# A two-phase MLP with block products: another assignment of tiles, input sums, squares and weight sums to engines

## The chip, the cores and the metric

The kernel runs on one core of a Trainium2 chip. The metric is the device time of one execution in microseconds (us), the median of several runs. PE (TensorE) multiplies, DVE (VectorE), ACT (ScalarE) and POOL (GpSimd) work element by element, SP (SyncE) issues transfers. PE writes into eight PSUM banks; POOL cannot read them.

## What is computed

A trunk of two layers on an input of 1024 rows by 1024 columns. Each layer has a mixer (attention of one kind or another), a norm, and an MLP. The change lies in the MLP and in the norm ahead of it:

```python
def rms_norm(x, g):
    y = xf * lax.rsqrt(jnp.mean(xf * xf, axis=-1, keepdims=True) + EPS)
    return (y * g).astype(x.dtype)

def sqrelu_mlp(xn, w1, w2):
    return jnp.square(jax.nn.relu(xn @ w1)) @ w2

for i in range(DEPTH):                       # 2 layers
    ...
    h = h + rms_norm(mix, g[1])
    f = sqrelu_mlp(rms_norm(h, g[2]), ffn_w1[i], ffn_w2[i])   # 1024 -> 4096 -> 1024
    h = h + rms_norm(f, g[3])
```

## The kernel before

**Precision.** Every fp32 operand of a product is split into a high part (rounded, by ACT) and a low part (the difference, by DVE or POOL), and each product is three matmuls: high x high, high x low, low x high. A low half can only be written after its high half.

**Two phases.** The hidden layer has 32 tiles of 128 columns. Phase one makes them (x @ w1, relu, square), phase two multiplies them by w2. Four tiles are made as plain products in `project_first` (two halves of 512 rows each, `th` 0 and 1); the other 28 come in 14 pairs. A pair is made as a 2x2 block product with seven products in place of eight (Strassen's scheme in Winograd's form): its operands are blocks of x and w1 and sums of blocks. `LOOPS = 6` turns of a loop make two pairs each (p = 0 into h_even, p = 1 into h_odd), and a peeled last turn makes the last two.

**Input sums.** x_sums holds four blocks: first four raw blocks of the transposed, normed input (high plus low: three made by POOL in `raw`, the fourth by DVE), then sums of them by DVE in place, then ACT's high and DVE's low halves of the four sums.

**Weights of phase one.** For each product k of a pair ACT writes the high half of its w1 operand (`up_high`) and POOL the low half (`up_low`); POOL also makes four sums of w1 blocks per pair. The halves go into a ring of eight slots; `w1_slot_free` says which product must be done before a slot is rewritten.

**Evacuation.** PE's products go round four banks. In `pair` DVE adds the seven products up into the four hidden blocks of the pair, frees the banks (`a_free`), squares each block by a fused op (max with 0, times itself), then makes three sums of squared blocks plus one in place: these are the seven block operands that phase two wants of a pair. SP stores all seven to h_operand_scratch. The squares and sums of a pair stand ahead of the next pair's evacuation in DVE's queue.

**Which tiles go where.** The four plain tiles and the first twelve pairs enter phase two as block operands: the plain tiles are put together into two pairs, with eight sums by DVE (`first_sum` into h_last_rows and h_more) before the loop. The last two pairs get no sums; their four tiles come last in phase two, as plain products (`down_last`).

**Phase two.** Products z = 0 to 27 in four groups g of seven (r = 0 to 6), four pairs deep in the first three groups and two in the last. For each z ACT copies the high half of the h operand and of the w2 operand, DVE the low half of h (`h_low`), POOL the low half of w2 (`down_low`); POOL also makes four sums of w2 blocks per group (`down_sum`). DVE takes PE's results into acc (`take`). The w2 operand buffers are three, so a half for z is written when product z-3 is done.

**The norm ahead** (`last_chunk_and_norm` on DVE, `norm` on ACT): DVE finishes the mixer's output (adds), scales it (y), adds the residual (h) and scales it for the MLP (xn); ACT makes the sums of squares and the roots. PE transposes the first 512 rows, runs the four tiles on them, transposes the last 512 and runs the four tiles again; ACT copies the high half of each transposed tile and DVE the low half.

Everything is ordered by semaphores; each engine runs its own queue in order. The order of operations is written out by hand.

## Time and profile before

| | |
|---|---|
| time, median of 3 runs | 2703.27 us (2702.24 to 2703.44) |
| the profiled execution | 2701.42 us, its span 2699.6 us |
| PE busy | 2454.9 us, 91% |
| DVE, POOL, ACT busy | 72%, 58%, 39% |
| mean granted clock of PE | 0.962 of full |

The profile comes from one execution. Its span starts at its first instruction; times below count from there. "Idle before" an instruction is the time in which its engine did nothing, and behind the arrow stands what ended it. The MLP of layer 0 lies at about 955 to 1635 us, that of layer 1 at 2009 to 2700 us.

### The profile page before, as it was taken

How to read it: one execution, taken by the hardware profiler on the slowest of the kernel's cores; microseconds unless marked ns; L12 is line 12 of the kernel's file. 1: busy time of each engine (PE TensorE's matmuls, PEld its weight loads, DVE VectorE, ACT ScalarE, POOL GpSimd, SP SyncE). 2: the span in 40 equal slices, each digit the busy share in tenths (PEclk: the TensorE clock that was granted, in tenths of full speed). 3: DMA queues.
4: the chain of work that ended last, by engine and by line, in shares of the span. 5: the costliest groups of instructions: out<-in, count | busy, mean ns of one | idle time of the engine just before them, and what ended most of it. 6: DMA issues, size and time to landing. Idle time of an engine off the chain costs nothing. (4 is left out here: it accounts for less than half of the span.)

```text
span 2699.6 us, 34715 instructions
## 1 busy us (share of the span) xinstructions
PE 2454.9 (91%) x11680; PEld 2017.9 (75%) x11680; DVE 1938.1 (72%) x3041; ACT 1046.8 (39%) x1785; POOL 1569.2 (58%) x833
## 2 busy tenths in 40 slices
PE   7899998898898987999999999977897999999998
PEld 6689877676776875888777887866775788878786
DVE  5599999766665588888755576165569788777666
ACT  5443533556554352122333235165544121233231
POOL 2112777545444156898877632366627698777951
PEclk9899989899999998999999999989998999999999
DMA  4471734543444623545644344654451554654343
GB/s 145 67 112 30 165 95 143 161 110 83 144 122 153 226 63 113 157 143 160 221 155 157 131 132 136 151 144 120 125 172 47 169 159 142 226 192 141 103 139 125
DMA packets 324033, 369.62 MB, mean 137 GB/s; under 512 B 14434, under 2 KB 222338, under 8 KB 321588
## 3 DMA queue, kind: packets, MB, share of 16 engines
q1 hardware_dynamic: 314404, 350.38, 44.3%
q10 hardware_dynamic: 9216, 16.78, 2.1%
q8 instruction: 83, 1.36, 0.2%
q0 software_dynamic: 272, 0.62, 0.1%
q14 instruction: 58, 0.48, 0.1%
HBM read 237.18 MB, written 130.55 MB: 136 GB/s over the span
## 5 line engine op out<-in xcount | busy, mean ns | idle before, releaser
L443 PE MATMUL ps<-xn_T,w_split 128*128 128x512 f32 (+1 forms) x2928 | 684.8, 393 | 32.4 <-DVE h_even L2264 30.8
L443 PEld LDWEIGHTS ps<-xn_T,w_split 128*128 128x128 f32 (+1 forms) x2928 | 551.7, 189 | 152.6 <-DVE h_even L2264 31.6
L443 PE MATMUL ps<-w_operand,h_operand 128*128 128x512 f32 x2016 | 468.1, 394 | 26.6 <-issue 17.0
L399 POOL TENSOR_TENSOR w_split<-w_raw,w_split 128x1024 fp32r<-128x1024 f32 x80 | 197.2, 2476 | 484.7 <-ACT w_split L392 484.4
L443 PEld LDWEIGHTS ps<-w_operand,h_operand 128*128 128x128 f32 x2016 | 383.6, 191 | 110.8 <-issue 29.0
L1193 POOL TENSOR_TENSOR w_split<-w_raw,w_split 128x512 fp32r<-128x512 f32 x168 | 271.9, 1643 | 74.5 <-ACT w_split L1670 74.5
L2315 DVE TENSOR_TENSOR acc<-acc,ps 128x512 f32<-128x512 f32 x288 | 186.1, 681 | 153.2 <-PE ps L443 152.7
L443 PE MATMUL ps<-x_sums_high,w_split 128*128 128x512 f32 x896 | 287.4, 392 | 4.3 <-POOL w_split L1193 4.3
L1225 POOL TENSOR_TENSOR w_operand<-w_block,w_operand 128x2048 fp32r<-128x2048 f32 x42 | 222.8, 5309 | 99.5 <-ACT w_operand L1690 99.5
L443 PE MATMUL ps<-w_split,hidden 128*128 128x512 f32 x960 | 224.7, 395 | 9.0 <-POOL w_split L399 6.3
L1677 ACT ACTIVATE h_operand<-h_operand_raw 128x2048 fp32r<-128x2048 f32 (+1 forms) x56 | 95.4, 1704 | 332.8 <-DMA h_operand_raw<-h_operand_scratch 332.8
L443 PEld LDWEIGHTS ps<-w_split,hidden 128*128 128x128 f32 x960 | 182.3, 191 | 48.7 <-issue 6.7
L443 PEld LDWEIGHTS ps<-x_sums_high,w_split 128*128 128x128 f32 x896 | 169.9, 190 | 40.7 <-ACT h_last_rows L1653 5.1
L2236 DVE TENSOR_TENSOR h_operand<-h_operand_raw,h_operand 128x2048 fp32r<-128x2048 f32 (+1 forms) x56 | 173.0, 3089 | 35.9 <-ACT h_operand L1677 35.6
L1670 ACT ACTIVATE w_split<-w_raw 128x512 fp32r<-128x512 f32 x168 | 99.4, 624 | 216.4 <-PE ps L443 201.6
L443 PE MATMUL ps<-w_split,unit_tile 128*128 128x512 f32 x576 | 158.9, 408 | 18.8 <-issue 7.4
L443 PE MATMUL ps<-x_sums_low,w_split 128*128 128x512 f32 x448 | 175.6, 392 | 0.0
L1959 DVE MATCH_REPLACE8 masks<-max,masks 128x1024 f32<-128x1024 f32 (+2 forms) x192 | 167.1, 880 | 0.1
L1955 DVE MAX8 max<-masks 128x8 f32<-128x1024 f32 (+2 forms) x192 | 161.4, 884 | 0.5 <-DVEq L1965 0.5
L443 PE MATMUL ps<-k_split,q_tile 128*128 128x192 f32 (+4 forms) x640 | 136.6, 340 | 23.1 <-DMA q_tile<-q_scratch 15.6
L2069 DVE TENSOR_TENSOR probs_T<-ps,probs_T 128x512 fp32r<-128x512 f32 x144 | 98.9, 688 | 75.5 <-ACT probs_T L1578 74.5
L1578 ACT ACTIVATE probs_T<-ps 128x512 fp32r<-128x512 f32 x144 | 83.9, 594 | 149.6 <-PE ps L2528 148.7
(249 smaller groups left out, 4333.4 us busy)
## 6 DMA issues: line engine op xcount, KB each, us to landing
h_operand_raw<-h_operand_scratch SPq DMA_DIRECT2D x42, 1024.0 KB, 5.2
w_raw<-in_w SPq DMA_DIRECT2D x72, 512.0 KB, 8.0
w_block<-in_w SPq DMA_DIRECT2D x48, 512.0 KB, 6.3
q_scratch<-q_split SPq DMA_DIRECT2D x128, 128.0 KB, 2.5
q_tile<-q_scratch ACTq DMA_DIRECT2D x64, 256.0 KB, 2.7
cat_scratch<-attn_out_split SPq DMA_DIRECT2D x128, 128.0 KB, 2.7
w_raw<-in_w_in SPq DMA_DIRECT2D x30, 512.0 KB, 5.0
h_operand_scratch<-h_even SPq DMA_DIRECT2D x14, 1024.0 KB, 4.5
```

Source lines behind the costliest of these rows:

```text
L399: nc.gpsimd.tensor_tensor(whl[:, n0 % 4, 1, :], wraw[:, n0 % 4, :], whl[:, n0 % 4, 0, :].bitcast(F32), ALU.subtract).then_inc(w_lo, 1)
L443: return nc.tensor.matmul(out_ap, stat, mov, start=start, stop=stop)
L1193: nc.gpsimd.tensor_tensor(w1_split(L, k, 1), w1_operand(L, k), w1_split(L, k, 0).bitcast(F32), ALU.subtract).then_inc(w1_lo, 1)
L1225: nc.gpsimd.tensor_tensor(w_split2(z, 1), w_operand2(z), w_split2(z, 0).bitcast(F32), ALU.subtract).then_inc(w2_lo, 1)
L1578: nc.scalar.activation(pT[:, x % 4, 0, :], ps[:, 4 + y % 2, :], ACT.Copy).then_inc(c_hi, 1)
L1670: nc.scalar.activation(w1_split(L, k, 0), w1_operand(L, k), ACT.Copy).then_inc(w1_hi, 1)
L1677: nc.scalar.activation(h_split(z, 0), h_split(z, 1, raw=True), ACT.Copy).then_inc(h2_hi, 1)
L1955: nc.vector.max(m8[:, e], rows[e]).then_inc(tk, 1)
L1959: nc.vector.match_replace(rows[e], m8[:, e], rows[e], NEG_SEL).then_inc(tk, 1)
L2069: nc.vector.tensor_tensor(pT[:, x % 4, 1, :], ps[:, 4 + y % 2, :], pT[:, x % 4, 0, :].bitcast(F32), ALU.subtract).then_inc(c_free, 1)
L2236: nc.vector.tensor_tensor(h_split(z, 1), h_split(z, 1, raw=True), h_split(z, 0).bitcast(F32), ALU.subtract).then_inc(h2_lo, 1)
L2315: last = nc.vector.tensor_tensor(e, e, o, ALU.add)
```

## The change

1. The four plain tiles come last in phase two, as plain products; all 14 pairs of phase one enter it as block operands. `first_sum` goes, SP moves the plain tiles with two stores in place of fourteen, the last two pairs get their squares and sums like the others, and the last one is put into h_end, a buffer of its own over the input sums. The rows of w2 are indexed accordingly.
2. POOL makes no input sum. DVE makes the raw block of the upper-left tiles inside the norm (`first_raw`) and the one of the lower-left after the transposes; ACT writes the other two straight from PSUM (`xn_raw`), reading the transposed tiles a second time, and PE waits for that before it overwrites their banks.
3. The squares of the pairs are ACT's: a relu and a square per block in place of DVE's fused op. DVE waits for them (h_sq), after the evacuation of the pair's last product.
4. w1's ring of halves has seven slots, and each is free when the product seven before is done.
5. In phase two POOL makes the sums of w2 in another order among themselves and against the low halves; SP loads w2's fourth block of group 0 after the second h operand.

```diff
-UP_RING = [-3, -3, -2, -2, -1, 0, 0, 0]
+UP_RING = [-3, -3, -2, -2, -1, -1, 0]
...
-        return w2[lay, (24 + j) * P:(25 + j) * P, :]
+        return w2[lay, (j - 4) * P:(j - 3) * P, :]
...
                 pe.wait_ge(a_free, f - 3)
+                if s % 2:
+                    pe.wait_ge(x_hi, 24 * (s // 2) + (9 if th else 1) + j)
                 project_half(FIRST[s] + j, f, th,
...
-        c = (k + 2 * L["tf"]) % 8
+        c = (k % 7 + 2 * L["tf"]) % 8
...
-        return up_group(L, k - 7 if k >= 8 else UP_RING[k])
+        return up_group(L, UP_RING[k] if first and k < 7 else k - 6)
...
-        raw(0, 0, 0)
-        raw(1, 0, 4)
-        pool.wait_ge(a_free, trans_pos(sn, 1, KT - 1) + 1)
-        raw(3, 1, 4)
-        head(0)
+        head(0, True)
...
+        def xn_raw(s, th, j):
+            for kt in range(4, KT):
+                f = trans_pos(s, th, kt)
+                act.wait_ge(a_free, f + 1)
+                nc.scalar.activation(xsum[:, j, kt - 4, :], ps[:, f % 4, :], ACT.Identity,
+                                     scale=gcol[:, s, kt:kt + 1]).then_inc(x_hi, 1)
...
             split_hi(act, FIRST[s] + 1)
+            if s % 2:
+                act.wait_ge(u_done, 3 * (s - 1) + 2)
+                xn_raw(s, 0, 1)
...
                 adds(7)
+                if s % 2:
+                    first_raw(s, 0)
                 stage_a(3)
+                if s % 2:
+                    first_raw(s, 1)
                 stage_b(2)
...
+        def squares_of(p, o, blocks, i, last=False):
+            act.wait_ge(a_free, up_group(L, 7 * p + o) + 1 + 14 * i)
+            n = 112 * lay + 8 * p + {1: 0, 5: 2, 6: 6}[o]
+            for j in blocks:
+                nc.scalar.activation(h_block(p, j, last), h_block(p, j, last), ACT.Relu).then_inc(h_sq, 1)
+            for m, j in enumerate(blocks):
+                act.wait_ge(h_sq, n + m + 1 + 16 * i)
+                nc.scalar.activation(h_block(p, j, last), h_block(p, j, last), ACT.Square).then_inc(h_sq, 1)
+
+        def round_(i, last=False):
+            for o in range(14):
+                if o < 7:
+                    up_high(7 + o, i)
+                elif not last:
+                    up_high(o - 7, i + 1)
+                if o % 7 == 1:
+                    squares_of(o // 7, 1, (1,), i, last)
+                if last and o == 12:
+                    down_high(0)
+                if o % 7 == 5:
+                    squares_of(o // 7, 5, (3, 0), i, last)
+                if o % 7 == 6:
+                    squares_of(o // 7, 6, (2,), i, last)
...
             nc.vector.tensor_tensor(b[1], b[0], o1, ALU.add).then_inc(a_free, 1)
-            done_to(1)
-            square(p, 1, i)
...
-            square(p, 3, i)
-            square(p, 0, i)
-            if not last:
-                ok_to(3)
-                nc.vector.tensor_tensor(b[0], b[1], b[0], ALU.subtract).then_inc(h_ok, 1)
...
+            nc.vector.tensor_tensor(b[2], b[2], m6, ALU.subtract).then_inc(a_free, 1)
+            squared(6)
+            nc.vector.tensor_tensor(b[0], b[1], b[0], ALU.subtract).then_inc(h_ok, 1)
+            sum_to(1)
+            nc.vector.tensor_tensor(b[4], b[3], b[0], ALU.subtract).then_inc(h_ok, 1)
+            sum_to(2)
+            nc.vector.tensor_tensor(b[5], b[4], b[1], ALU.add).then_inc(h_ok, 1)
+            squared(8)
+            nc.vector.tensor_tensor(b[6], b[4], b[2], ALU.subtract).then_inc(h_ok, 1)
...
-        sp.wait_ge(h0_ok, 18 * lay + 18)
+        sp.wait_ge(x_hi, 24 * lay + 24)
+        for th in range(2):
+            sp.dma_start(hopd[lay, 14 + th, 0:4].rearrange("k r t -> r k t"), (first_rows, last_rows)[th][:]).then_inc(h0_mv, 16)
...
             down_low(z)
+            if g == 0:
+                down_low(z + 1)
             pool.wait_ge(w2_ld[1], w_loads(lay, g))
             pool.wait_ge(w2_ld[3], w_loads(lay, g))
             down_sum(g, 0, b12, b22, b12, ALU.subtract)
-            if g == 0:
-                down_low(z + 1)
-            down_sum(g, 1, b11, b12, b11, ALU.add)
             if g:
                 down_low(z + 1)
             down_low(z + 2)
-            down_sum(g, 2, b21, b11, b21, ALU.subtract)
+            down_sum(g, 1, b11, b12, b11, ALU.add)
             down_low(z + 3)
-            down_sum(g, 3, b22, b22, b11, ALU.subtract)
-            for r in range(4, 7):
-                down_low(z + r)
+            down_sum(g, 2, b22, b22, b11, ALU.subtract)
+            down_low(z + 4)
+            down_sum(g, 3, b21, b11, b21, ALU.subtract)
+            down_low(z + 5)
+            down_low(z + 6)
```

**How the instructions move.** DVE, layer 0, from its input sums to the end of what stands ahead of the loop of pairs. Before:

```order
L2219 TENSOR_TENSOR x_sums<-x_sums 128x1024 x4
L2210 TENSOR_TENSOR h_last_rows<-h_first_rows,h_last_rows 128x512
L2219 TENSOR_TENSOR x_sums<-x_sums 128x1024 x4
L2210 TENSOR_TENSOR h_last_rows<-h_first_rows,h_last_rows 128x512
L2227 TENSOR_TENSOR x_sums_low<-x_sums,x_sums_high_89 128x1024 x2
L2227 TENSOR_TENSOR x_sums_low<-x_sums,x_sums_high_91 128x1024 x2
L2210 TENSOR_TENSOR h_last_rows<-h_last_rows 128x512
L2210 TENSOR_TENSOR h_last_rows<-h_last_rows,h_first_rows 128x512 x2
L2227 TENSOR_TENSOR x_sums_low<-x_sums,x_sums_high_92 128x1024 x2
L2227 TENSOR_TENSOR x_sums_low<-x_sums,x_sums_high_90 128x1024 x2
L2210 TENSOR_TENSOR h_last_rows<-h_last_rows 128x512
L2210 TENSOR_TENSOR h_more<-h_last_rows,h_first_rows 128x512 x2
```

and after the change, from the low halves of the second transposes on:

```order
L1786 TENSOR_SCALAR xn<-acc,rstd_b 128x8x128 x2
L1906 SCALAR_TENSOR_TENSOR xn_T<-ps,gain_cols,xn_T 128x512 x8
L2334 TENSOR_TENSOR x_sums<-xn_T 128x1024 x2
L2244 TENSOR_TENSOR x_sums<-x_sums 128x1024 x8
L2252 TENSOR_TENSOR x_sums_low<-x_sums,x_sums_high_89 128x1024 x2
L2252 TENSOR_TENSOR x_sums_low<-x_sums,x_sums_high_91 128x1024 x2
L2252 TENSOR_TENSOR x_sums_low<-x_sums,x_sums_high_92 128x1024 x2
L2252 TENSOR_TENSOR x_sums_low<-x_sums,x_sums_high_90 128x1024 x2
```

The eight operations on h_last_rows and h_more are gone from between the sums and the low halves, and the low halves follow the sums directly.

ACT, layer 0, end of phase one and start of phase two (w_operand and h_operand are phase two's operands; the number tells the buffer). Before:

```order
L1670 ACTIVATE w_split<-w_split_raw 128x512
L1670 ACTIVATE w_split<-w_raw 128x512 x4
L1690 ACTIVATE w_operand_107<-w_block_113 128x2048
L1677 ACTIVATE h_operand_101<-h_operand_raw_104 128x2048
L1690 ACTIVATE w_operand_108<-w_block_115 128x2048
L1677 ACTIVATE h_operand_102<-h_operand_raw_105 128x2048
L1677 ACTIVATE h_operand_103<-h_operand_raw_106 128x2048
```

and after the change:

```order
L1721 ACTIVATE h_even<-h_even 128x512
L1724 ACTIVATE h_even<-h_even 128x512
L1721 ACTIVATE h_end<-h_end 128x512
L1724 ACTIVATE h_end<-h_end 128x512
L1689 ACTIVATE w_operand_108<-w_block_114 128x2048
L1676 ACTIVATE h_operand_102<-h_operand_raw_105 128x2048
L1721 ACTIVATE h_end<-h_end 128x512 x2
L1724 ACTIVATE h_end<-h_end 128x512 x2
L1721 ACTIVATE h_end<-h_end 128x512
L1724 ACTIVATE h_end<-h_end 128x512
L1689 ACTIVATE w_operand_109<-w_block_116 128x2048
L1676 ACTIVATE h_operand_103<-h_operand_raw_106 128x2048
```

The high half of the second w2 operand (w_operand_108 before, w_operand_109 now) stands behind the relus and squares of the last pair.

POOL, layer 0, the first group of phase two and the start of the second. L1225 (L1218 now) writes a low half, L1231 (L1224 now) a sum of w2 blocks; blocks 113 to 116 are 114 to 117 in the changed kernel. Before:

```order
L1225 TENSOR_TENSOR w_operand_107<-w_block_113,w_operand_107 128x2048
L1231 TENSOR_TENSOR w_block_114<-w_block_116,w_block_114 128x2048
L1225 TENSOR_TENSOR w_operand_108<-w_block_115,w_operand_108 128x2048
L1231 TENSOR_TENSOR w_block_113<-w_block_114,w_block_113 128x2048
L1225 TENSOR_TENSOR w_operand_109<-w_block_114,w_operand_109 128x2048
L1231 TENSOR_TENSOR w_block_115<-w_block_113,w_block_115 128x2048
L1225 TENSOR_TENSOR w_operand_107<-w_block_116,w_operand_107 128x2048
L1231 TENSOR_TENSOR w_block_116<-w_block_116,w_block_113 128x2048
L1225 TENSOR_TENSOR w_operand_108<-w_block_116,w_operand_108 128x2048
L1225 TENSOR_TENSOR w_operand_109<-w_block_115,w_operand_109 128x2048
L1225 TENSOR_TENSOR w_operand_107<-w_block_113,w_operand_107 128x2048
L1225 TENSOR_TENSOR w_operand_108<-w_block_113,w_operand_108 128x2048
```

and after the change:

```order
L1218 TENSOR_TENSOR w_operand_108<-w_block_114,w_operand_108 128x2048
L1218 TENSOR_TENSOR w_operand_109<-w_block_116,w_operand_109 128x2048
L1224 TENSOR_TENSOR w_block_115<-w_block_117,w_block_115 128x2048
L1218 TENSOR_TENSOR w_operand_110<-w_block_115,w_operand_110 128x2048
L1224 TENSOR_TENSOR w_block_114<-w_block_115,w_block_114 128x2048
L1218 TENSOR_TENSOR w_operand_108<-w_block_117,w_operand_108 128x2048
L1224 TENSOR_TENSOR w_block_117<-w_block_117,w_block_114 128x2048
L1218 TENSOR_TENSOR w_operand_109<-w_block_117,w_operand_109 128x2048
L1224 TENSOR_TENSOR w_block_116<-w_block_114,w_block_116 128x2048
L1218 TENSOR_TENSOR w_operand_110<-w_block_116,w_operand_110 128x2048
L1218 TENSOR_TENSOR w_operand_108<-w_block_114,w_operand_108 128x2048
L1218 TENSOR_TENSOR w_operand_109<-w_block_114,w_operand_109 128x2048
```

In group 0 every sum now stands one low half later than before, and in the second group the second low half stands ahead of the second sum. The sums of blocks 115 and 116 have changed places: the sixth low half reads the sum that is now made last.

## Rows read from the trace of the kernel before

**Rows 1.** the page's part 1: busy us (share of the span) xinstructions
```profile
PE 2454.9 (91%) x11680; PEld 2017.9 (75%) x11680; DVE 1938.1 (72%) x3041; ACT 1046.8 (39%) x1785; POOL 1569.2 (58%) x833
```

**Rows 2.** PE's waits, whole span: engine, what waits, releaser: us in total, times, longest
```profile
PE ps L558 <- DVE xn L1763: 34.1, 3, 15.9
PE ps L443 <- DVE h_even L2264: 30.8, 2, 15.4
```

**Rows 3.** PE's timeline, start of layer 0's MLP: start, us, instruction xcount [idle before]
```profile
954.91 22.04 PE L443 MATMUL ps<-xn_T,w_split 128*128 128x512 f32 x96 [0.49 <-DVE xn_T L1871]
986.07 6.28 PE L558 MATMUL ps<-ident,xn 128*128 128x128 f32 x32 [9.12 <-DVE xn L1763]
992.17 27.48 PE L443 MATMUL ps<-xn_T,w_split 128*128 128x512 f32 x120
1021.84 0.59 PE L443 MATMUL ps<-x_sums_high,w_split 128*128 128x512 f32 x1 [2.19 <-POOL w_split L1193]
...
1044.55 5.25 PE L443 MATMUL ps<-xn_T,w_split 128*128 128x512 f32 x12 [15.38 <-DVE h_even L2264]
```

**Rows 4.** DVE's timeline, the norm in front of that MLP
```profile
967.10 4.62 DVE L1783 SCALAR_TENSOR_TENSOR acc<-acc,rstd_a,gain_rows 128x1024 f32<-128x1024 f32 x2
971.64 6.76 DVE L1794 TENSOR_TENSOR acc<-acc,h_in 128x1024 f32<-128x1024 f32 x2
978.32 5.58 DVE L1763 TENSOR_SCALAR xn<-acc,rstd_b 128x1024 f32<-128x1024 f32 x2
...
984.60 1.42 DVE L1763 TENSOR_SCALAR xn<-acc,rstd_b 128x1024 f32<-128x1024 f32 x2
```

**Rows 5.** POOL's timeline, the same stretch
```profile
970.60 12.76 POOL L1184 TENSOR_TENSOR x_sums<-xn_T 128x1024 f32<-128x1024 f32 x4
```

**Rows 6.** DVE's timeline, where the input sums begin and where phase one's first evacuation stands
```profile
1001.16 6.99 DVE L2219 TENSOR_TENSOR x_sums<-x_sums 128x1024 f32<-128x1024 f32 x4 [2.28 <-POOL x_sums L1184]
...
1043.82 0.68 DVE L2264 COPY h_even<-ps 128x512 f32<-128x512 f32 x1
```

**Rows 7.** DVE's groups, 994 to 1044.5 us: xcount | busy, mean ns | idle
```profile
L2227 DVE TENSOR_TENSOR x_sums_low<-x_sums,x_sums_high 128x1024 fp32r<-128x1024 f32 x8 | 15.7, 2014 | 0.0
...
L2210 DVE TENSOR_TENSOR h_last_rows<-h_last_rows 128x512 f32<-128x512 f32 x2 | 3.5, 1756 | 0.0
L2210 DVE TENSOR_TENSOR h_last_rows<-h_last_rows,h_first_rows 128x512 f32<-128x512 f32 x2 | 3.4, 1716 | 0.0
L2210 DVE TENSOR_TENSOR h_more<-h_last_rows,h_first_rows 128x512 f32<-128x512 f32 x2 | 3.3, 1690 | 0.0
L2210 DVE TENSOR_TENSOR h_last_rows<-h_first_rows,h_last_rows 128x512 f32<-128x512 f32 x2 | 2.5, 1232 | 0.0
```

**Rows 8.** tile x_sums: duration ns min/median/max, first and last start
```profile
L2219 DVE TENSOR_TENSOR x_sums<-x_sums x16: 1210/2303/2318, 1001.2 to 2070.9; 128x1024 f32<-128x1024 f32 x16
```

**Rows 9.** tile h_first_rows: ScalarE's square, ns min/median/max
```profile
L1655 ACT ACTIVATE h_first_rows<-h_first_rows x8: 629/630/630, 980.5 to 2038.3; 128x512 f32<-128x512 f32 x8
```

**Rows 10.** all engines, phase one at speed: us, busy (xcount) by engine, PEclk, DMA
```profile
1064.00:1292.00 228.00, 228.00 (x1008) 188.79 (x1006) 186.90 (x189) 51.20 (x85) 198.05 (x132) 1.00 0.52 154
```

**Rows 11.** ACT's groups in the same stretch
```profile
L1670 ACT ACTIVATE w_split<-w_split_raw 128x512 fp32r<-128x512 f32 x12 | 7.6, 633 | 84.1 <-POOL w_split_raw L1189 84.1
```

**Rows 12.** PE's timeline, hand-over from phase one to two, layer 0
```profile
1316.03 5.71 PE L443 MATMUL ps<-w_operand,h_operand 128*128 128x512 f32 x24 [2.33 <-DVE acc L2313]
```

**Rows 13.** PE's timeline, the same hand-over in layer 1
```profile
2374.70 79.19 PE L443 MATMUL ps<-w_operand,h_operand 128*128 128x512 f32 x336 [6.48 <-DVE acc L2313]
```

**Rows 14.** POOL's groups, 1302 to 1360 us, first products of phase two
```profile
L1225 POOL TENSOR_TENSOR w_operand<-w_block,w_operand 128x2048 fp32r<-128x2048 f32 x5 | 27.6, 5524 | 2.0 <-ACT w_operand L1690 2.0
L1231 POOL TENSOR_TENSOR w_block<-w_block,w_block 128x2048 f32<-128x2048 f32 x4 | 24.9, 6233 | 6.3 <-DMA w_block<-in_w 6.3
```

**Rows 15.** PE's timeline, the three holes between groups of phase two
```profile
1399.70 20.58 PE L443 MATMUL ps<-w_operand,h_operand 128*128 128x512 f32 x80 [5.50 <-issue]
...
1482.56 17.76 PE L443 MATMUL ps<-w_operand,h_operand 128*128 128x512 f32 x70 [4.26 <-issue]
...
2537.56 32.74 PE L443 MATMUL ps<-w_operand,h_operand 128*128 128x512 f32 x136 [6.70 <-issue]
```

**Rows 16.** POOL's timeline in front of the first of them
```profile
1381.69 11.39 POOL L1231 TENSOR_TENSOR w_block<-w_block,w_block 128x2048 f32<-128x2048 f32 x2
1393.04 11.10 POOL L1225 TENSOR_TENSOR w_operand<-w_block,w_operand 128x2048 fp32r<-128x2048 f32 x2
```

235 lines of the change are left out of this document (96 added, 139 removed).

## The prediction

> **What bounds the kernel now.** I read the page's busy shares first, then PE's waits, then the timelines of PE, DVE and POOL around each wait. PE is busy 91% of the span [rows 1], and the change neither adds nor removes a matmul, so it can only give or take PE's holes. The 128x512 matmuls run back to back wherever nothing holds them: in the steady part of phase one PE is busy 228.00 of 228.00 us with 1008 of them, 0.226 us each, at a granted clock of 1.00, the 2.4 GHz level [rows 10]. So a product of 12 is 2.71 us, a first-tile half of 24 is 5.43, and a product of phase two (48) is 10.86. The holes that touch the change stand in four places, the first three once per layer:
> (a) Before the second transposes PE waits 9.1 us for DVE's scaled rows (two of the three waits in 34.1 us) [rows 2, 3].
> (b) Four products into phase one, PE waits 2.2 us for POOL's low half and then 15.4 us for DVE, which comes to its first evacuation only at 1043.82 [rows 2, 3, 6].
> (c) At the hand-over to phase two PE waits for DVE 2.3 us in layer 0 and 6.5 in layer 1 [rows 12, 13].
> (d) Inside phase two there are three holes of 5.50, 4.26 and 6.70 us [rows 15] that the profile calls issue. The first ends where the first of POOL's two low halves must end: POOL writes two weight sums (11.39 us) and only then the low half that the second product of the group needs [rows 16].
>
> **The change part by part, (a).** Today POOL adds four raw input sums from 970.60 to 983.36 [rows 5]. While it does, DVE's y, h and xn take 2.31, 3.38 and 2.79 us each; xn takes 0.71 once POOL is quiet [rows 4]. A sum of the same width takes 1.21 alone and 2.30 beside POOL [rows 8]. Now DVE and ScalarE alone make these sums. I price y and h at 1.21 and xn at 0.71 with POOL quiet, one y still at 2.3 because POOL's last weight split stays: 2.3+1.2+2.4+1.4 = 7.3 us for two y, two h and two xn that took 16.96. The remaining ScalarE root and two xn add about 3 us. All rows are then ready some 9 to 10 us earlier, at 977 instead of 986.0, which is when PE's first half ends (954.91+22.04). The two raw sums that DVE takes over (2 x 1.21) fall into its two waits for ScalarE's roots, ahead of 967.10. So hole (a) goes to about 0. What is late next is ScalarE.
> The Trainium skill, page "SBUF — State Buffer", section "Who interferes with whom", says why: an instruction of VectorE with two SBUF inputs, or in a 2-port mode, and one of GpSimd exclude each other for a whole instruction. The drop of xn from 2.79 to 0.71 us agrees. If the slow times were instead DVE's own, hole (a) would stay; that is rival C.
>
> **(a), what is added on PE's path.** ScalarE reads the upper four transposed tiles once more (4 ops per half), and PE's first product in that bank waits for it. An op of this width takes 0.63 us there [rows 9]. First half: +0.7 us. Second half: the reads stand behind all eight high copies, so PE starts about 8.0 us after its first transpose instead of 6.1 (992.17-986.07) [rows 3]: +1.9.
>
> **(b).** Between its last transposed tile and its first evacuation DVE now runs 26 ops, among them eight sums of first tiles, 12.7 us in all [rows 7]. These go, since the first four tiles are no longer part of the block sums. The wait for POOL's raw sums (2.28 us) [rows 6] goes too. What remains on DVE is 2 raw sums, 8 sums, 8 lows: 10 x 1.21 with POOL quiet, then 8 x 2.0 beside POOL's low halves [rows 7] = 28.1 us. PE meanwhile has 4 half tiles and 4 products, 21.7+10.9 = 32.6 us. DVE has about 8 us of transposed tiles in front of it, just as PE has, so it arrives 4 us before PE needs the fifth bank: the 15.4 goes, at least to 0 to 2. As for the 2.2 us for POOL: from the second half tile on, two ScalarE ops and two copies (2.5 us) and six POOL ops of at most 2 us stand in front of the low half of the third product, 14.5 us, and PE reaches that product 16.3 us behind the tile (2 x 5.43 + 2 x 2.71). So it goes as well.
> Sum of (a) and (b), from the end of the first half (976.95) to the start of the fifth product: now 1044.55-976.95 = 67.6 us; then 0.7+8.0+21.7+10.9 = 41.3. That saves 26.3. Behind the hole the first 12 matmuls take 5.25 us in place of 2.71 [rows 3], another 2.5. **28.8 us a layer, 57.6 for both.** Bounds: 20 (half of the DVE lows late) to 31.
>
> **Steady phase one.** Per pair of products four fused squares leave DVE and eight ops of 0.63 us come to ScalarE, 5.0 us in a pair of 19.0; ScalarE is busy 51 of 228 us now, DVE 187 [rows 10]. DVE's block sums now wait for ScalarE's squares, and the next pair's evacuation stands behind those sums in DVE's queue. Worked out from the sixth product's end: DVE 1.4, ScalarE 2.6, then the seventh product, four sums: DVE is free 4.3 us after the pair's last product, or 7 if POOL doubles the sums. PE needs the first bank of the next pair 10.2 us after it. So it costs nothing while 3 to 6 us of slack stand. In the first pair ScalarE is held by POOL's weight sum, which is behind there: **0 to 2 us, I take 1 a layer, 2 for both.** The ring of weight halves is 7 deep in place of 8, or 4 to 6 at the loop's turn, and POOL has 30 of 228 us to spare: nothing.
> The Trainium skill, "ScalarE: Activation LUTs", section "Rules for kernel authors", says that relu belongs on VectorE. Here it would be right for the op by itself: relu and square are 1.26 us on ScalarE against one fused op. If it held for the path too, rival D is what it would do here, with its own price; by the slack above it shows only in the last pair of a layer.
>
> **(c) The hand-over** gets worse. Today POOL makes the first weight sum while phase one ends. Now its second low half comes first, and that waits for a ScalarE copy which stands behind the last squares: about 5 us (bounds 3 to 8) after phase two starts. From there to the low half of the sixth product are nine POOL ops and three hand-overs through ScalarE. Nine ops took 52.5 us, 5.83 each, and a hand-over 2.0 [rows 14]. So 5+52.5+6 = 63.5 us, and PE wants it after 5 x 10.86 = 54.3: 9 us of holes in place of 2.3 and 6.5. At 5.0 us an op and an early start it is 2, at 8 us start 12. DVE has sums in the last pair too, but POOL is idle just then. **Cost 9.4 us for both; bounds -5 to +15.**
>
> **(d)** In later groups the second low half moves ahead of the second sum, one POOL op, about 5.7 us (11.39/2) [rows 16]. 5.50+4.26+6.70 = 16.5 of holes become 0 to 1 each: **gain 15.4**, bounds 11 to 16.5. The sixth product's low half gets one hand-over (2.0) more but has 3 us to spare.
>
> Moves that cost nothing: 14 small stores of first tiles become 2, and both pairs of the end store seven blocks, 0.75 MB more each while PE multiplies; the fourth w2 block is loaded behind the second h operand on SP's queue, which only follows the order of use. The eight small loads of the last tiles become two and go one product later, with eight products still before ScalarE copies them.
> Sum: 57.6 - 2 - 9.4 + 15.4 = 61.6 us. From the profiled execution's 2701.42 (span 2699.6) that is 2639.8; the median is 1.85 higher, 2703.27, so **2641.6 us**.
>
> **Rivals.**
> A, POOL's chain is the new bound: hand-overs cost 12 us each layer (15 worse than now, not 9.4), the holes of (d) keep 2 us each, and the first pairs 2. 57.6-4-15+10 = 48.6: 2655. For it: POOL's 5.83 mean [rows 14]; against: DVE has fewer two-input ops there.
> B, everything fits: hand-over no worse than today, 57.6-0-0+16 = 73.6: 2630. For it: POOL is idle when the last squares run, and DVE's sums then cost 0.7 us each.
> C, hole (a) stays, because y, h and xn are slow by themselves: 6.4 us less per layer (9.1 less the part that ScalarE's four first-tile squares now take anyway), 2654.
> D, slower than before: the handshake of DVE and ScalarE. In the steady part ScalarE waits 7.0 us per pair for POOL's weight sum (84.1 us in 12) [rows 11]. Should that wait fall in front of the third and first squares, DVE is free at 11 to 13 us instead of 4.3 to 7 and PE, which decides at 10.2, stops in every one of 28 pairs: at 2.5 us a pair 70 us, 2712. Against: the sum in question is made two to four products earlier, since POOL starts it when product 2 ends.
> E, the order is as written but DVE's first lows are slowed to 2.3 and start late, so that the 15.4 shrinks only to 6: 2653.
>
> **How the numbers follow.** Forecast 60%, 2630 to 2652 by its bounds; A 13%; B 8%; C 7%; E 6%; D 3%; the rest 3% lies beyond, on the good side. Range **2624 to 2663**. This kernel's measurement can tell 0.2%, 5.4 us, from no change. Faster 0.96, same 0.01, slower 0.03.
>
> **What would show it.** Right: no PE wait for xn over 2 us before the second transposes; PE starts the second half about 8 us behind its first transpose; no wait for h_even at the fifth product; xn, y and h at 0.7 and 1.2 us; 228-like full busy PE in phase one; holes of 2 to 12 us, ended by POOL's w_operand, within the first six products of phase two; none over 1 us at the second product of a later group. Wrong: a wait of PE for an h block in every pair (D), or xn still at 2.8 us with POOL quiet (C).

## The result and the profile after

The changed kernel takes **2620.52 us** (median of 4 runs, 2619.45 to 2623.67) against 2702.76 for the kernel before beside it (2698.99 to 2703.44): ratio 0.970, 95% interval 0.9684 to 0.9717. The forecast was 2641.6 in a range of 2624 to 2663: the sign was right, the gain of 82 us was 20 more than the 61.6 forecast, and the time lies 3.5 us below the range. A second measurement (e11 below) gave 2624.14 (2621.12 to 2627.58), ratio 0.9715 (0.9699 to 0.9731), so the low end of the range is where the kernel stands; the centre was 17 to 21 us off.

I cut the span at four points of PE's timeline: A is from the first matmul of an MLP's input projection to the first of phase two, B from there to the next norm's first projection (in layer 1 to the end), M lies between the two MLPs. The first five columns are differences of such row starts, in us; the last two are the profiled execution's span and the median of all executions.

| kernel | A, layer 0 | B, layer 0 | M | A, layer 1 | B, layer 1 | span | median |
|---|---|---|---|---|---|---|---|
| before | 347.7 | 332.7 | 373.9 | 347.9 | 342.4 | 2699.6 | 2702.8 |
| changed | 318.2 | 321.1 | 370.7 | 318.3 | 332.9 | 2617.6 | 2620.5 |
| changed, again (e11) | 318.2 | 322.1 | 372.3 | 318.3 | 333.0 | 2622.4 | 2624.1 |
| e1 raw sums on GpSimd | 333.4 | 320.8 | 372.3 | 333.9 | 330.2 | 2647.8 | 2648.4 |
| e4 eight first sums added | 331.2 | 323.7 | 372.2 | 329.0 | 332.8 | 2644.2 | 2646.5 |
| e8 four first sums added | 323.5 | 323.7 | 371.5 | 323.9 | 331.3 | 2630.0 | 2630.5 |
| e2 squares on VectorE | 320.0 | 323.4 | 372.2 | 321.1 | 333.0 | 2626.0 | 2628.1 |
| e3 old weight order | 318.2 | 340.4 | 371.6 | 320.0 | 348.7 | 2655.1 | 2656.2 |
| e7 first group's old start | 318.2 | 324.4 | 372.3 | 318.2 | 333.1 | 2620.7 | 2623.4 |
| e5 before, new order alone | 347.9 | 321.5 | 371.8 | 347.8 | 327.5 | 2673.5 | 2675.1 |

Of the 82.0 us between the two spans 59.1 are in the two A, 21.3 in the two B (20.1 by the second measurement), and 1.6 in M and what lies ahead of the first MLP together. M is anything from 370.7 to 374.1 in the experiments, and e5, which changes nothing there, has 371.8 where the kernel before has 373.9, so its 3.2 are no effect of the change. PE's timeline of the changed kernel at the start of layer 0's MLP, to be laid beside [rows 3]:

```profile
956.48 22.05 PE L442 MATMUL ps<-xn_T,w_split 128*128 128x512 f32 x96 [1.30 <-ACT x_sums L1309]
...
981.24 2.63 PE L559 MATMUL ps<-ident,xn 128*128 128x128 f32 x16 [0.97 <-DVE xn_T L1906]
985.32 27.49 PE L442 MATMUL ps<-xn_T,w_split 128*128 128x512 f32 x120 [1.45 <-ACT x_sums L1309]
```

The hole of 9.12 us ahead of the second transposes is gone, ScalarE's second reading of the transposed tiles adds the waits of 1.30 and 1.45, and behind them the next row with an idle time of any size is the first of phase two (0.78); 2.19 and 15.38 are gone too. VectorE's timeline in the norm, beside [rows 4], and where phase one's first evacuation stands, beside [rows 6, 7]:

```profile
968.74 2.48 DVE L1806 SCALAR_TENSOR_TENSOR acc<-acc,rstd_a,gain_rows 128x1024 f32<-128x1024 f32 x2
971.14 2.35 DVE L1825 TENSOR_TENSOR acc<-acc,h_in 128x1024 f32<-128x1024 f32 x2
973.41 1.41 DVE L1786 TENSOR_SCALAR xn<-acc,rstd_b 128x1024 f32<-128x1024 f32 x2
```

```profile
997.51 16.89 DVE L2252 TENSOR_TENSOR x_sums_low<-x_sums,x_sums_high 128x1024 fp32r<-128x1024 f32 x8
1014.32 0.68 DVE L2286 COPY h_even<-ps 128x512 f32<-128x512 f32 x1
```

y, h and xn take 1.24, 1.18 and 0.71 us each (2.31, 3.38, 2.79 before), and the evacuation starts at 1014.32 instead of 1043.82. PE's waits over the whole span (total, times, longest), beside [rows 2], and its timeline at the two hand-overs, beside [rows 12, 13]; there is no hole between the groups of phase two where [rows 15] had three:

```profile
PE ps L442 <- issue: 14.9, 3, 7.6
...
PE ps L442 <- DVE acc L2325: 6.8, 2, 3.4
...
PE ps L442 <- ACT x_sums L1309: 5.5, 4, 1.4
```

```profile
1274.70 11.18 PE L442 MATMUL ps<-w_operand,h_operand 128*128 128x512 f32 x48 [0.78 <-DVE h_operand L2257]
1289.27 90.92 PE L442 MATMUL ps<-w_operand,h_operand 128*128 128x512 f32 x387 [3.39 <-DVE acc L2325]
```

```profile
2299.32 45.44 PE L442 MATMUL ps<-w_operand,h_operand 128*128 128x512 f32 x192 [3.40 <-DVE acc L2325]
2346.82 63.46 PE L442 MATMUL ps<-w_operand,h_operand 128*128 128x512 f32 x272 [2.06 <-issue]
```

### The profile page after: what moved, and what is told of

Read it like the earlier page. It is cut to its first block, busy times and chain, and to the rows that moved or that the text cites. A ratio compares the mean times of both kernels' runs of the same rounds, so it can differ in the third digit from the quotient of the medians.

```text
span 2617.6 us, 34947 instructions
## 1 busy us (share of the span) xinstructions
PE 2432.2 (93%) x11680; PEld 1999.3 (76%) x11680; DVE 1761.4 (67%) x2933; ACT 1189.7 (45%) x2025; POOL 1471.8 (56%) x821
## 4 chain that ended last, share of the span: by engine, by line
PE 66%; issue 14%; DVE 9%; POOL 5%; ACT 4%; DMA 2%; DVEq 1%; SPq 0%; POOLq 0%; ACTq 0%
PE ps L442 63%; POOL attn_out_split L1164 2%; POOL attn_out L1162 2%; PE ps L2528 1%; DVE masks L1994 1%; DVE max L1990 1%; DVE probs_T L2104 1%; DVE logits L2069 1%; DVE masks L1973 1%; POOL attn_out_split L1160 1%; DMA h_operand_raw<-h_operand_scratch 1%; ACT relu_scores L1426 1%; ACT probs_T L1577 1%; POOL attn_out_low L1157 1%; DVE acc L1806 1%
## 5 line engine op out<-in xcount | busy, mean ns | idle before, releaser
L1186 POOL TENSOR_TENSOR w_split<-w_raw,w_split 128x512 fp32r<-128x512 f32 x168 | 241.8, 1450 | 104.9 <-ACT w_split L1669 103.4
L1218 POOL TENSOR_TENSOR w_operand<-w_block,w_operand 128x2048 fp32r<-128x2048 f32 x42 | 207.8, 4947 | 111.4 <-ACT w_operand L1689 111.4
L2257 DVE TENSOR_TENSOR h_operand<-h_operand_raw,h_operand 128x2048 fp32r<-128x2048 f32 (+1 forms) x56 | 167.5, 2991 | 52.8 <-ACT h_operand L1676 52.5
L1669 ACT ACTIVATE w_split<-w_raw 128x512 fp32r<-128x512 f32 x168 | 104.9, 629 | 167.4 <-PE ps L442 163.8
```

Of the source, the lines that this page charges most:

```text
L1186: nc.gpsimd.tensor_tensor(w1_split(L, k, 1), w1_operand(L, k), w1_split(L, k, 0).bitcast(F32), ALU.subtract).then_inc(w1_lo, 1)
L1218: nc.gpsimd.tensor_tensor(w_split2(z, 1), w_operand2(z), w_split2(z, 0).bitcast(F32), ALU.subtract).then_inc(w2_lo, 1)
L1669: nc.scalar.activation(w1_split(L, k, 0), w1_operand(L, k), ACT.Copy).then_inc(w1_hi, 1)
L2257: nc.vector.tensor_tensor(h_split(z, 1), h_split(z, 1, raw=True), h_split(z, 0).bitcast(F32), ALU.subtract).then_inc(h2_lo, 1)
```

## The experiments

Each run is compared with runs of the kernel before on the same chip (medians 2699.2 to 2703.0). "Over the changed kernel" counts from its first measurement, 2620.5; from the second, 2624.1, each such number is 3.6 us less.

**Part (a), who makes the raw input sums.** e1 gives the six raw sums of a layer back to GpSimd:

```diff
+        raw(0, 0, 0)
+        raw(1, 0, 4)
...
+        raw(3, 1, 4)
...
-                xn_raw(s, 0, 1)
...
-        xn_raw(sn, 1, 3)
...
-                    first_raw(s, 0)
...
-                    first_raw(s, 1)
```

> The changed kernel, but the six raw input sums of a layer are on GpSimd again, where the kernel before had them; everything else stays. Theory S (GpSimd's sums held up VectorE's norm work): the y, h and xn rows of VectorE that took 2.48, 2.35 and 1.41 for two go back to about twice to three times that, PE's gap ahead of the second half's transposes grows from 6.8 to 14 to 15 us in each layer, and the time is 2620.5 + 2 x 7.9 = 2636 us (2633 to 2640). Rival C (those rows were slow for another reason, or the second half was late for another reason): gap stays near 7, time 2619 to 2622.

Measured: 2648.41, ratio 0.980 (0.978 to 0.982), 28 us over the changed kernel. VectorE's norm rows and PE's timeline of e1:

```profile
969.37 4.62 DVE L1813 SCALAR_TENSOR_TENSOR acc<-acc,rstd_a,gain_rows 128x1024 f32<-128x1024 f32 x2
973.92 6.74 DVE L1832 TENSOR_TENSOR acc<-acc,h_in 128x1024 f32<-128x1024 f32 x2
980.58 5.59 DVE L1793 TENSOR_SCALAR xn<-acc,rstd_b 128x1024 f32<-128x1024 f32 x2
```

```profile
988.35 6.18 PE L557 MATMUL ps<-ident,xn 128*128 128x128 f32 x32 [9.11 <-DVE xn L1793]
...
1026.12 0.79 PE L442 MATMUL ps<-x_sums_high,w_split 128*128 128x512 f32 x1 [4.15 <-POOL w_split L1184]
```

The rows are those of [rows 4] again, 4.62, 6.74 and 5.59, with nothing changed in these steps themselves: GpSimd's sums made them slow, and rival C is out. The hole is back (9.11), and a second one that I had not counted, 4.15 for GpSimd's low half, since its first weight sums now stand behind the raw ones. Per layer: holes of 9.1 and 4.15, less the 0.97 and 1.45 that go with ScalarE's reads, are 10.8 us; A grew by 15.2 and 15.7. The other 4.4 and 4.9 us are matmuls that take longer behind a hole: the granted clock is 0.50 from 988 to 992 us and again from 1026 to 1030. The time lies 8 us over the 2640 at which my range ended, since I had counted neither the second hole nor this.

**Part (b), the sums of the first tiles.** e4 puts eight unused VectorE sums where the kernel before had those of the first tiles, e8 four:

```diff
+        extra(0)
         x_sum_op(3, 3, 0, ALU.subtract, s0)
...
+        extra(2, 3, 4)
         x_sum_low(19, 3)
         x_sum_low(21, 1)
+        extra(5, 6, 7)
```

> The changed kernel with work added: eight VectorE sums of 128x512 in each layer at the places where the kernel before had the sums of the first four tiles (one and one among the x sums, three and three among the low parts). Their results are not used. Theory B1 (these sums, in VectorE's order ahead of the first product's copy, made the first pair wait): the copy that starts at 1014.3 comes 5.6 us (8 x 0.7) to 12.7 us (the four rows of before) later; PE has 3 us to spare there, so it waits 3 to 10 us ahead of the fifth product in each layer: 2626 to 2640 us, most likely 2634. Rival B2 (the slow low parts under GpSimd were all of it): 2620 to 2622.

> As e4_first_sums_added, with four extra VectorE sums of 128x512 in place of eight (one ahead of each of the four places). Each of the four left out took 1.74 us there, 7 us in all, of a hole of 8.88 us, so 1.9 us of hole is left in each layer. In e4 the stage grew by 12.9 us for that hole, so 4.0 us were slower matmuls. Theory L (the loss at a lower granted clock comes only behind long holes): 2620.5 + 2 x 1.9 = 2624 us (2622 to 2627). Theory A (any hole at that place costs the same 4 us behind it): 2632 us (2630 to 2635).

Measured: e4 2646.51, ratio 0.9808 (0.9785 to 0.9832), 26 us over the changed kernel; e8 2630.51, ratio 0.9743 (0.9728 to 0.9758), 10 us over. VectorE and PE in e4, and PE in e8:

```profile
1007.87 3.48 DVE L2342 TENSOR_TENSOR spare<-h_first_rows 128x512 f32<-128x512 f32 x2
...
1023.54 3.41 DVE L2342 TENSOR_TENSOR spare<-h_first_rows 128x512 f32<-128x512 f32 x2
1026.88 0.68 DVE L2288 COPY h_even<-ps 128x512 f32<-128x512 f32 x1
```

```profile
1027.61 5.14 PE L444 MATMUL ps<-xn_T,w_split 128*128 128x512 f32 x12 [8.88 <-DVE h_even L2288]
```

```profile
1020.32 4.61 PE L444 MATMUL ps<-xn_T,w_split 128*128 128x512 f32 x12 [2.48 <-DVE h_even L2288]
```

These sums, at 1.7 us each beside GpSimd, make the first pair wait (B1). The holes came out as expected (8.88 expected 3 to 10; 2.48 expected 1.9), the times did not: in e4 A grew by 12.9 and 10.7 us for holes of 8.9 and 9.2, in e8 by 5.3 and 5.7 for holes of 3.5 (the 2.48 and 1.0 more ahead of phase two's first product) and 2.2. They are not the whole of the 15.38 us of before. GpSimd's raw sums are likely to be most of the rest: e1 and e4, each run by itself, put back 28.1 and 26.4 us together (layer 0, layer 1) of the 29.5 that A gained. e4 in stretches of 10 us (PE busy, count, granted clock):

```profile
1005.00:1015.00 10.00, 10.00 (x46) 1.00 0.51 188
1015.00:1025.00 10.00, 3.73 (x17) 0.85 0.47 129
1025.00:1035.00 10.00, 7.39 (x23) 0.64 0.00 1
1035.00:1045.00 10.00, 10.00 (x46) 1.00 0.00 0
```

The stretch that holds the hole's end has a granted clock of 0.64 on average; from 1027.6 to 1031 it is 0.50, the 1.2 GHz level. The twelve matmuls of the first product take 5.14 us behind 8.88 us of idle and 4.61 behind 2.48, and 2.9 where the clock is 1.00. So the loss depends little on the hole's length: 2.3 and 1.7 us (layer 1: 1.5 and 1.4) in these twelve, and 2.5 and 1.9 (1.6 and 1.9) in the whole of A. That is theory A of e8, with a smaller sum. Another 1.6 us is chance: the 120 matmuls of the second half take 27.5 or 29.1 us in one layer or the other of several kernels, behind the same gap of 1.45 us; in e4 the granted clock behind it is 0.86 from 985 to 995.

**Part (d) and the hand-over, the order of GpSimd's weight sums.** e3 puts the whole old order into the changed kernel, e7 only its start in the first group, e5 the new order alone into the kernel before. From e3:

```diff
             down_sum(g, 0, b12, b22, b12, ALU.subtract)
+            if g == 0:
+                down_low(z + 1)
+            down_sum(g, 1, b11, b12, b11, ALU.add)
             if g:
                 down_low(z + 1)
             down_low(z + 2)
-            down_sum(g, 1, b11, b12, b11, ALU.add)
```

> The changed kernel, but GpSimd makes the second phase's weight sums in the order of the kernel before, in all four groups. Theory: the three holes of 5.50, 4.26 and 6.70 us come back as they were (16.5 us) with 1 to 3 us of slower matmuls behind them, and at the hand-over the low part of the second product comes one sum later, by 6.6 us, of which GpSimd's idle 8.65 us ahead of it can swallow most: 0 to 8 us in all. Sum 2638 to 2648 us, most likely 2641. By the prediction's own term (15.4 for the holes alone): 2636. Rival: the holes were not of this order's making and stay away: 2621.

> The changed kernel, but in the first group GpSimd makes the first weight sum ahead of the second product's low part, as it does in the other groups; the new order of the other sums stays. Theory: the hand-over wait is 7.5 us as in the kernel with the whole old order (there 7.48 and 7.54, put down to GpSimd's w_operand) instead of 3.4, the 2.06 at the sixth product goes, and slower matmuls add 1 to 2 us a layer: 2620.5 + 4.1 + 2.5 + 3 = 2630 us (2626 to 2633). Rival, the prediction's own reckoning (the hand-over is set by when GpSimd ends its nine steps, which this order leaves as it is): 2620 to 2623.

> The kernel before, with the new order of GpSimd's second-phase weight sums alone. Undoing this order in the changed kernel cost 35.7 us: holes of 13.9 between the groups, 8.1 more at the two hand-overs, less 2.1, and slower matmuls behind the holes (5.3 and 3.8 us in the two stages). Theory K: in the kernel before, the hand-over is set by VectorE (2.33, 0.79 and 6.48 us of waits for acc), so only the 16.5 us of holes between the groups and some 5 us of slower matmuls go: 2702.6 - 21.5 = 2681 us (2677 to 2687). Additive rival: the whole 35.7 goes here too: 2667 us (2664 to 2672).

Measured: e3 2656.18, ratio 0.9834 (0.9813 to 0.9854), 36 us over the changed kernel. e7 2623.42, ratio 0.9721 (0.9706 to 0.9736): the same as the changed kernel. e5 2675.10, ratio 0.9913 (0.9898 to 0.9928): 24 us gained by the order alone. PE in e3, layer 0:

```profile
1293.06 79.82 PE L442 MATMUL ps<-w_operand,h_operand 128*128 128x512 f32 x336 [7.48 <-POOL w_operand L1218]
1378.34 2.05 PE L442 MATMUL ps<-w_operand,h_operand 128*128 128x512 f32 x4 [5.46 <-issue]
```

```profile
1461.97 67.17 PE L442 MATMUL ps<-w_operand,h_operand 128*128 128x512 f32 x288 [4.42 <-issue]
```

and in e5, layer 0:

```profile
1317.38 5.68 PE L443 MATMUL ps<-w_operand,h_operand 128*128 128x512 f32 x24 [1.41 <-DVE acc L2314]
...
1364.89 15.45 PE L443 MATMUL ps<-w_operand,h_operand 128*128 128x512 f32 x60 [2.05 <-issue]
```

The holes of [rows 15] are the order's doing. Apart from the start of the first group, which they share, e3 and e7 differ only in it: 9.9 us of holes in layer 0, while B differs by 16.0; in layer 1 10.2 and 15.7. In the kernel before, all waits of PE in B sum to 13.2 us in layer 0 and 13.4 in layer 1 (those of [rows 12, 13, 15] and small ones of 0.79, 0.30 and 0.21); in e5 to 4.6 and 3.2. That is 8.6 and 10.2 less, and B falls by 11.2 and 14.9. Again a hole was worth 1.3 to 3 us more than its length. The kernel before shows this too: in the first 20 us behind the three holes of [rows 15] PE makes 79, 81 and 81 matmuls, where it makes 88 at a granted clock of 1.00. e7 has a hand-over wait of 7.48 in place of 3.4 and is not measurably slower: B is 2 to 3 us longer in layer 0 and the same in layer 1, where the wait at the sixth product is gone in return. My 2630 was wrong there, and so was the 2638 to 2648 for e3, which had both the hand-over (a wait of 7.5 us in each layer) and the slower matmuls too small. e5 fell between its two theories, just under the range of the first.

Why layer 1's hand-over gained too is in the timelines of the kernel before, VectorE's squares of the last pair and GpSimd's first sum:

```profile
2356.06 5.71 DVE L2232 SCALAR_TENSOR_TENSOR h_odd<-h_odd 128x512 f32<-128x512 f32 x2
...
2362.40 4.41 DVE L2232 SCALAR_TENSOR_TENSOR h_odd<-h_odd 128x512 f32<-128x512 f32 x1
```

```profile
2356.43 4.78 POOL L1231 TENSOR_TENSOR w_block<-w_block,w_block 128x2048 f32<-128x2048 f32 x1 [5.99 <-DMA w_block<-in_w]
```

Three squares that take 0.65 us elsewhere took 10.1: the first two beside GpSimd's sum of 4.78 us, the third beside its next instruction, a low half of 5.07 us begun at 2361.18. In layer 0 only the third was caught (4.40 us). The new order starts GpSimd later, when they are done; in e5 the same three take 2.0.

**Squares on ScalarE.** e2 gives them back to VectorE:

```diff
-                    squares_of(o // 7, 1, (1,), i, last)
...
+            square(1)
```

> The changed kernel, but the squares of relu in the pairs are fused steps of VectorE again (four of 128x512 in a pair), not ScalarE's. Theory: they bring nothing by themselves, since VectorE has room in the steady phase (186.9 busy of 228 before) and the two ways to the last sums of a pair are about as long (at the hand-over ScalarE's squares end 1279.3 and VectorE's sums 1280.9; on VectorE 1276.4 + 3 x 0.7 + 4 x 0.7 = 1281.3): 2618 to 2624 us. Rival: VectorE was close to its limit and the squares on ScalarE carry part of the gain: 5 us or more slower than the changed kernel, with PE waiting for h_even or h_odd. Rival D of the prediction, turned round (the handshake with ScalarE costs): faster than 2617.

Measured: 2628.11, ratio 0.9732 (0.9715 to 0.975), 4 to 8 us over the changed kernel: neither the theory's 4 at most nor the rival's place. PE's waits for an h block are 0.24 us; some 5 us of the loss are in the two A (1.6 of them the chance of above), and 1.3 to 2.4 in B of layer 0, at the hand-over, where VectorE's last sums met GpSimd. The two measurements of the changed kernel lie 3.6 us apart themselves, so the size of this loss is not well known. VectorE and GpSimd of e2; PE's wait at the second product was 7.34 us for 3.39:

```profile
1280.67 4.99 DVE L2301 TENSOR_TENSOR h_end_sums<-h_end 128x512 f32<-128x512 f32 x1
1285.69 4.92 DVE L2303 TENSOR_TENSOR h_end_sums<-h_end_sums,h_end 128x512 f32<-128x512 f32 x1
```

```profile
1280.11 5.00 POOL L1218 TENSOR_TENSOR w_operand<-w_block,w_operand 128x2048 fp32r<-128x2048 f32 x1 [12.27 <-ACT w_operand L1689]
1285.07 5.00 POOL L1224 TENSOR_TENSOR w_block<-w_block,w_block 128x2048 f32<-128x2048 f32 x1
```

Two sums of 0.7 us take as long as the GpSimd instruction beside each. With the squares on ScalarE VectorE's last sum ends at 1280.85, and GpSimd starts at 1281.15, 0.3 us later. Is it the length of one instruction that counts? e9 and e10 cut each GpSimd step of the first group in four, e9 in the changed kernel, e10 in e2:

```diff
+                for k in range(4):
+                    last = nc.gpsimd.tensor_tensor(lo[:, k], raw[:, k], hi[:, k], ALU.subtract)
```

> As e2_squares_vector (squares on VectorE), with GpSimd's steps of the first group in four instructions each. In e2 two VectorE sums of 128x512 took 4.99 and 4.92 us beside one GpSimd instruction each. Theory W: they take 0.7 plus at most 1.3 each, under 2.0 us, PE's wait of 7.34 us at the hand-over falls to 2 to 4, and the time from 2628.1 to 2619 to 2624. Rival B: they stay near 5 us and the time at 2628.

> The changed kernel, but each of GpSimd's steps of the first group of phase two (128x2048) is four instructions of 128x512. Theory W (a VectorE step with all its operands in SBUF waits until the whole GpSimd instruction that runs has ended): the h_operand low part that took 5.02 us at the hand-over takes 2.3 plus one wait of at most 1.3, so 2.5 to 3.6 us, PE's wait there falls from 3.4 to 1 to 2 us, and the time is 2617 to 2621 us, since GpSimd's chain takes some of it back. Rival B (the two engines share the port by bandwidth, whatever the instructions' length): the low part stays near 5 us and the wait at 3.4.

VectorE of e10, at the same two sums:

```profile
1283.77 1.68 DVE L2311 TENSOR_TENSOR h_end_sums<-h_end 128x512 f32<-128x512 f32 x1
1285.49 1.67 DVE L2313 TENSOR_TENSOR h_end_sums<-h_end_sums,h_end 128x512 f32<-128x512 f32 x1
```

4.99 and 4.92 became 1.68 and 1.67: VectorE waits for one whole instruction of GpSimd (theory W). But the times went the other way: e10 2637.24, ratio 0.9764 (0.9747 to 0.9781); e9 2634.95, ratio 0.9755 (0.9738 to 0.9771). PE of e9:

```profile
1292.24 12.57 PE L442 MATMUL ps<-w_operand,h_operand 128*128 128x512 f32 x48 [2.37 <-DVE acc L2335]
1308.35 23.62 PE L442 MATMUL ps<-w_operand,h_operand 128*128 128x512 f32 x96 [3.54 <-issue]
1334.43 11.17 PE L442 MATMUL ps<-w_operand,h_operand 128*128 128x512 f32 x48 [2.47 <-issue]
```

The wait for acc fell from 3.4 to 2.4, and new ones of 3.5 and 2.5 came behind it: a GpSimd step takes 5.0 or 7.05 us in four pieces where it took 4.63 or 6.67 in one. The likely reason for the 7.05 is that now each piece can wait for VectorE; no run shows it by itself. GpSimd's low half for the sixth product ends 67.7 us after phase two's start, where it ended at 60.0. Here the long instruction is the better one, because GpSimd's chain is the bound. e12 adds to e9 VectorE's copy of the first quarter ahead of its low part (e6 below). I expected 2616 to 2620 us; it took 2631.76, ratio 0.9748 (0.9732 to 0.9764), with waits of 2.4, 5.0 and 2.6 in layer 0, so it fails for the same reason.

**What the rest of the change costs at the hand-over.** By e5 the order alone leaves 321.5 and 327.5 us in the two B; the changed kernel has 321.1 and 332.9 (again: 322.1 and 333.0). GpSimd's chain in the changed kernel, layer 1 (phase two starts at 2284.75), and its first step in e5 (start 2346.03):

```profile
2291.20 4.63 POOL L1218 TENSOR_TENSOR w_operand<-w_block,w_operand 128x2048 fp32r<-128x2048 f32 x1 [8.69 <-ACT w_operand L1689]
2295.78 6.59 POOL L1224 TENSOR_TENSOR w_block<-w_block,w_block 128x2048 f32<-128x2048 f32 x1
2304.40 4.63 POOL L1218 TENSOR_TENSOR w_operand<-w_block,w_operand 128x2048 fp32r<-128x2048 f32 x1 [2.03 <-ACT w_operand L1689]
...
2342.15 4.57 POOL L1218 TENSOR_TENSOR w_operand<-w_block,w_operand 128x2048 fp32r<-128x2048 f32 x1 [2.02 <-ACT w_operand L1689]
```

```profile
2348.70 4.62 POOL L1225 TENSOR_TENSOR w_operand<-w_block,w_operand 128x2048 fp32r<-128x2048 f32 x1 [9.41 <-ACT w_operand L1691]
```

The chain starts 6.45 us after phase two in one and 2.67 in the other, since ScalarE's copy of the second product's weights now stands behind the last squares, and ends 62.0 after it. e6 changes VectorE's order only (first quarter copied out ahead of the second low part); e13 moves the weights' copy ahead of the squares; e15 also puts VectorE's last four sums behind the products; e14 is e15 with e6; e16 is e15 with both copies ahead.

```diff
                 if last and o == 12:
                     down_high(0)
+                    down_high(1)
```

> The changed kernel, but VectorE copies the first quarter of the first down product out of PSUM before it makes the low part of the second product's h operand, not after. Theory: at the hand-over PE waits for that copy (3.4 us), which starts 4.9 us late because the low part ahead of it stands behind one whole GpSimd instruction; with the copy first PE can go when the low part ends, 1289.27 - 1287.9 = 1.0 to 1.4 us earlier in each layer; in the second layer GpSimd's chain takes it back at the sixth product (its wait of 2.06 grows by as much). 2619 to 2620 us against 2620.5, holes of 2.1 to 2.4 in place of 3.4. Rival: the wait is for GpSimd's low part of the weights and nothing moves: 3.4 stays.

> The changed kernel itself once more, beside the other three: 2620.5 us (2618 to 2624); the part between the two MLPs, 370.7 us in its first profile and 373.9 in that of the kernel before, falls anywhere in 370.5 to 374, as it did in the experiments (371.5 to 372.3). Rival (the change shortens that part): it stays within 0.3 of 370.7.

> The changed kernel, but at the end of phase one ScalarE makes the high copy of the second product's weights ahead of the last three squares, not behind them. Theory S (the chain's start costs): GpSimd starts 1277.5 - 1274.7 = 2.7 to 3.5 us after phase two instead of 6.45 and the wait of 2.06 at the sixth product goes; but VectorE's last four sums now fall beside GpSimd's instructions and wait for whole ones, 4.6 to 5 us each for two or more of them, as in e2, so the hand-over wait grows from 3.4 to 7 us or more, and the time is 2621 to 2627. Rival (the chain's start is of no account, VectorE not touched): 2620 to 2624 with the wait at 3.4.

> As e13, and VectorE makes the last pair's four block sums one each behind the second to fifth down product, where they are not urgent (their store and the reload of the first tiles on SyncE's queue come four products later). Theory S: the chain still starts at 3 us, nothing of VectorE's stands in front of the second low part, so the hand-over wait stays 3.4 and the wait at the sixth product is gone; GpSimd's chain ends 3.4 us earlier: 2 us less in each layer than the changed kernel (2620.5 and 2624.1 in its two measurements): 2616 to 2620. Rival: the four late sums stand behind GpSimd's instructions, hold up VectorE's low parts, and PE waits 2 us or more in several of the first six products: 2624 or more.

> As e15, with VectorE's copy of the first quarter of the first down product ahead of the second low part, as in e6. With GpSimd's chain 3.4 us earlier its wait at the sixth product no longer takes back what the earlier copy gives: another 1.3 us in each layer: 2613 to 2618, at best 0.3% under the changed kernel. Rival: as for e15.

> As e15_late_sums, but ScalarE makes both high copies of the second product (weights and h operand) ahead of the last three squares. Theory S: VectorE's low part is ready about 78.7 - 72.9 = 5.8 us after phase two starts in place of 8.9 and stands behind one GpSimd instruction only (ends near 11), so PE's wait of 5.38 at the second product falls to 0 to 1, and one of up to 2 at the sixth product comes back: 3 to 4 us less in each layer: 2613 to 2617. Rival (the h operand is not landed that early, or another wait takes the place): 2620 to 2622.

e17 is e16 with VectorE's copy first, as in e6; I expected 2611 to 2617 us, or 2620 and more if VectorE's low part missed its turn.

Measured, medians and ratios: e6 2620.12, 0.9708 (0.9695 to 0.9721); e13 2625.02, 0.9712 (0.9697 to 0.9727); e15 2621.13, 0.9698 (0.9685 to 0.9711); e14 2621.89, 0.9698 (0.9685 to 0.9712); e16 2622.75, 0.9714 (0.970 to 0.9728); e17 2623.95, 0.972 (0.9707 to 0.9734). None can be told from the changed kernel's 0.970 and 0.9715. So e13 came out by its theory S (its hand-over waits are 7.71 and 6.90), and the gains that I expected of e15, e14, e16 and e17 did not come. PE, VectorE and GpSimd of e15:

```profile
1289.50 90.84 PE L443 MATMUL ps<-w_operand,h_operand 128*128 128x512 f32 x390 [5.38 <-DVE acc L2343]
```

```profile
1281.89 6.27 DVE L2262 TENSOR_TENSOR h_operand<-h_operand_raw,h_operand 128x2048 fp32r<-128x2048 f32 x1 [7.21 <-ACT h_operand L1678]
```

```profile
1276.86 4.64 POOL L1220 TENSOR_TENSOR w_operand<-w_block,w_operand 128x2048 fp32r<-128x2048 f32 x1 [6.12 <-ACT w_operand L1693]
1281.43 4.58 POOL L1226 TENSOR_TENSOR w_block<-w_block,w_block 128x2048 f32<-128x2048 f32 x1
```

GpSimd starts 3.9 us after phase two (1272.94), as wanted, but VectorE's low part, ready 0.5 us after GpSimd's next step had begun, stands 6.3 us, and the wait at the second product is 5.38 for 3.39. In e16 that wait is 0.83, and four others follow (0.81, 0.78, 2.06, 0.57); its sixth product starts 2.8 us earlier in layer 1 than the changed kernel's (59.3 us after phase two's start, for 62.1), and its B there is only 0.3 to 0.4 us shorter, in layer 0 not shorter at all. So the late start costs some 3 us up to the sixth product, and taking it away gives nothing in the end. B in layer 1 of e5 is 5.4 us shorter than the changed kernel's. 3.7 of it are there by the start of its sixth product (58.35 for 62.1). The other 1.6 are in the 20 us behind the same hole of 2.06 us; here the changed kernel, then e5:

```profile
2346.82:2366.82 20.00, 20.00 (x81) 0.92 0.61 211
```

```profile
2404.38:2424.38 20.00, 20.00 (x88) 1.00 0.63 211
```

The granted clock fell behind this hole in one and not in the other, and so it does among the other runs: in e11 it fell in layer 1 and not in layer 0. What decides it stays open, and these 1.6 us are no gain of e5's.

## Why the prediction was right and where it failed

**Right.** Hole (a) went for the reason given: xn at 0.71 with GpSimd quiet, e1 brings 9.11 back. The second half starts 6.8 us after the first ends (forecast 8.7). VectorE reaches the first evacuation in time (the lows took 16.9 us for the 16 forecast), and e4 shows that the first tiles' sums had held it up. From there on phase one is without a hole: the first pairs cost 0, not 1 a layer. A gave 59.1 us. ScalarE's reads put its start off by 0.8 us in each layer (waits of 1.30 and 1.26 for 0.49 and 0.52), which leaves 57.5; the sum had 57.6-2 = 55.6. The holes of (d) went to 0, by the order alone. Rivals A, C, D and E are out; the handshake of D shows nowhere. Rival B, "everything fits", came nearest, and its condition, a hand-over no worse than before, is what the trace shows; the prediction gave it 8%, and 3% to a time below the range. Not run by themselves were the ring of seven slots and the moves on SyncE's queue; phase one's rows show no wait that would point to them.

**The step that failed is the pricing of phase two, terms (c) and (d): -9.4 and +15.4, 6.0 in all, where the two B gave 21.3 (again: 20.1).** PE's holes in the two B fall from 26.6 to 8.9 us. By them the 15.3 us between forecast and result divide into 9.4 of (c), 1.1 of (d), 1.3 of small waits that I had not counted (0.79, 0.30 and 0.21), and 3.5 of matmuls that no longer run slower behind a hole (21.3 less 17.7).
- (c), 9.4, is the larger miss. Its holes are 3.4 us in layer 0 and 5.5 in layer 1, 8.9 in all for the 8.8 of [rows 12, 13]: it cost nothing. GpSimd's chain started later than forecast (6.45 us for 5), but its nine steps took 5.28 and 5.49 us on average (layer 0, layer 1) for my 5.83, so it ended at 60.0 and 62.0, not at 63.5. And I compared its end with a PE at full clock, 54.3 us, where PE took 57.7 and 56.6 for these five products without the holes (the sixth starts at 61.1 and 62.1). The wait that does stand in both layers, 3.4 us at the second product, is not the chain's: it ends with VectorE's copy, behind a low part that takes 5.02 us beside GpSimd. Against the order alone (e5) B is the same in layer 0 and 5.4 longer in layer 1.
- (d), 15.4, counted the three holes at their length. For (b) I had added 2.5 us for the matmuls that run at the lower clock behind the hole, and here I forgot it. e5 shows the term: 18.8 us of holes and 7.3 us of slower matmuls, 26.1 in B and 24 in the median. In the changed kernel part of it is lost again behind its own holes, which leaves the 3.5.
- The order also holds a gain that I had not seen. In layer 1 the old one began GpSimd's first sum beside VectorE's last squares (10.1 us for three); the new one does not. I had read the 6.48 of [rows 13] as a price that stays.

So (c) had the length of GpSimd's steps and PE's pace wrong, and (d) left out what the clock does behind a hole. Of the 20.4 us between 82.0 and 61.6, 15.3 are in B, 1.9 in A, and 3.2 in M, which is chance. The range was too narrow on the good side, since the bounds of (d), 11 to 16.5, were drawn from lengths of holes alone, and rival B was priced with the same fault.

**Two rules that the prediction drew on.** In e2 a VectorE sum took 4.99 us beside one GpSimd instruction of 5.00, in e10 1.68 beside GpSimd instructions of a quarter of the width. The Trainium skill, page "SBUF — State Buffer", section "Who interferes with whom", says that a VectorE instruction with two SBUF inputs and a GpSimd instruction that reads SBUF exclude each other; the two runs agree. With relu and square back on VectorE (e2) the kernel took 4 to 8 us longer. The Trainium skill, page "ScalarE: Activation LUTs", section "Rules for kernel authors", says that relu belongs on VectorE; for this path it did not hold.

## What to carry to other kernels

Price a hole in front of matmuls at its length plus the slower matmuls behind it, and read those from the rows after it (here mostly 1.3 to 3 us, for holes of 3.3 us as for 9; behind holes of 1.45 and 2.06 us it was either 1.6 or almost nothing, by run and layer). When work is moved off GpSimd or VectorE, look at what instruction of the other engine is running when each short step starts: a step of 0.7 us can take 5, and 0.3 us of order decides it. And when two chains end at about the same time, bringing one forward moves the wait and not the end: six variants of the hand-over changed where PE waited and not the time.

## What the runs showed of the hardware

- A VectorE sum of 128x512 with its operands in SBUF took 4.99 us beside one GpSimd instruction of 5.00 (e2) and 1.68 beside shorter ones of 128x512 (e10); three squares of the last pair took 10.1 us in the kernel before and 2.0 with GpSimd later (e5). A VectorE sum with one operand in PSUM took 0.68 in the same stretch of the kernel before, at 2361.69, inside a GpSimd instruction of 5.07.
- GpSimd pays as well: a step of 128x2048 takes 4.6 us alone and 6.6 to 6.7 where VectorE's low part falls beside it (changed kernel), and 5.0 or 7.05 in four pieces (e9).
- What the lower granted clock costs behind a hole does not scale with the hole: 12 matmuls took 5.14 us behind 8.88 us of idle (e4), 4.61 behind 2.48 (e8), 2.9 with none. It does not even come each time: behind the same hole of 2.06 us PE made 81 matmuls in 20 us at 0.92 in the changed kernel and 88 at 1.00 in e5.
